# PEER in a two-layer diffusion step: rows run tile by tile, and table two's rows are summed two at a time in 64x64 tiles

## What is computed

```python
q = (xt @ wq).reshape(T, 8, 2, 128)                       # 8 heads, two halves
s1, s2 = q[:, :, 0] @ k1.T, q[:, :, 1] @ k2.T             # 128 scores each
v1, i1 = top_k(s1, 16); v2, i2 = top_k(s2, 16)
sc, pos = top_k(v1[..., :, None] + v2[..., None, :], 16)  # of 256 sums
eid = chosen i1 * 128 + i2; gate = softmax(sc)
act = gelu(sum_d x[t] * u_tab[eid])                       # table one
out[t] = sum over 8 heads x 16 of (gate * act) * v_tab[eid]   # table two
```

## Time and profile before

| what | us or share |
|---|---|
| median of the runs | 2608.44 |
| the profiled execution | 2606.61 |
| its span, first to last instruction | 2604.7 |
| PE, matmul busy | 2125.3 (82%) |
| DVE busy | 1598.7 (61%) |
| POOL busy | 948.2 (36%) |
| ACT busy | 486.4 (19%) |
| gathers (queue q0) | 805.36 MB, 74.7% of the 16 DMA engines' span |

### The profile page before, as it was taken

The page is one execution under the profiler, slowest core; times in us unless marked ns, Lnnn a source line. Parts: engine busy times, 40 slices in busy tenths (PEclk is TensorE's granted clock), DMA queues, the critical chain, the costliest instruction groups (busy, mean ns, idle before and its releaser), DMA issues.

```text
span 2604.7 us, 20351 instructions
## 1 busy us (share of the span) xinstructions
PE 2125.3 (82%) x6324; PEld 1044.5 (40%) x6324; DVE 1598.7 (61%) x4191; ACT 486.4 (19%) x1337; POOL 948.2 (36%) x775
## 2 busy tenths in 40 slices
PE   5998688697969787887899996797969688888777
PEld 2554433242424333433347654342424233334333
DVE  3234576767766677776432435777666677676764
ACT  2251211111111111111242112111111111111112
POOL 0000264444545444454100003544545444454541
PEclk9999699898989898998889997998989898999989
DMA  9993699999999999999723117999999999999994
GB/s 303 318 328 112 276 406 419 420 418 421 417 417 418 410 418 412 408 420 419 268 73 98 61 37 294 421 418 421 418 421 418 421 418 413 418 409 415 417 421 184
DMA packets 215769, 913.24 MB, mean 351 GB/s; under 512 B 19664, under 2 KB 116176, under 8 KB 116848
## 3 DMA queue, kind: packets, MB, share of 16 engines
q0 software_dynamic: 110592, 805.36, 74.7%
q1 hardware_dynamic: 97840, 101.20, 12.1%
q10 hardware_dynamic: 7232, 5.39, 0.7%
HBM read 909.26 MB, written 2.63 MB: 350 GB/s over the span
## 4 chain that ended last, share of the span: by engine, by line
PE 42%; DMA 41%; DVE 6%; POOL 5%; issue 3%; ACT 2%; SPq 0%; DVEq 0%; ACTq 0%
DMA slab<-in_peer_uv,idx 28%; PE psum L717 24%; PE psum L643 8%; DMA arena<-in_peer_uv,idx 8%; POOL slab L313 3%; POOL arena L313 2%; DMA slab<-in_ada_w 2%; DMA area<-in_peer_wq 2%; PE psum L681 2%; PE psum L819 2%; PE psum L608 2%; DVE slab L1077 2%; PE psum L897 1%; PE psum L758 1%; ACT diag L459 1%
## 5 line engine op out<-in xcount | busy, mean ns | idle before, releaser
L717 PE MATMUL psum<-arena,diag 128*128 128x512 f32 x2304 | 1087.6, 632 | 368.6 <-ACT diag L459 368.6
L313 POOL DMA_INDIRECT arena<-in_peer_uv,idx x576 | 698.9, 1213 | 1530.7 <-PE psum L717 879.6
L717 PEld LDWEIGHTS psum<-arena,diag 128*128 128x128 f32 x2304 | 459.9, 203 | 984.4 <-issue 984.4
L1077 DVE SCALAR_TENSOR_TENSOR arena<-arena,xtok 128x1024 f32<-128x1024 f32 x576 | 687.0, 1223 | 268.4 <-DMA arena<-in_peer_uv,idx 262.7
L1077 DVE SCALAR_TENSOR_TENSOR slab<-slab,xtok 128x1024 f32<-128x1024 f32 x192 | 235.4, 1228 | 227.4 <-DMA slab<-in_peer_uv,idx 227.4
L717 PE MATMUL psum<-slab,diag 128*128 128x512 f32 x768 | 337.4, 593 | 0.0
L313 POOL DMA_INDIRECT slab<-in_peer_uv,idx x192 | 245.3, 1278 | 71.5 <-issue 39.3
L459 ACT ACTIVATE diag<-ident,wts 128x128 f32<-128x128 f32 x768 | 235.0, 389 | 107.8 <-DVE wts L1098 107.4
L643 PE MATMUL psum<-arena,slab 128*128 128x384 f32 x672 | 227.8, 497 | 7.1 <-DVE arena L1147 4.9
L450 ACT ACTIVATE tanh<-inner 128x8 f32<-128x8 f32 (+1 forms) x98 | 20.3, 207 | 1140.5 <-DVE inner L1084 1140.5
L717 PEld LDWEIGHTS psum<-slab,diag 128*128 128x128 f32 x768 | 146.2, 190 | 183.4 <-issue 183.4
(11 more groups left out here) (222 smaller groups left out, 1482.2 us busy)
## 6 DMA issues: line engine op xcount, KB each, us to landing
slab<-in_ada_w SPq DMA_DIRECT2D x33, 1024.0 KB, 8.3
area<-in_peer_wq SPq DMA_DIRECT2D x16, 1024.0 KB, 25.4
slab<-in_gla_w_in SPq DMA_DIRECT2D x12, 1024.0 KB, 5.4
arena<-in_peer_uv,idx POOLq DMA_INDIRECT x576, 17.1
keys<-in_ada_w SPq DMA_DIRECT2D x8, 1024.0 KB, 9.2
area<-in_ada_w SPq DMA_DIRECT2D x7, 1024.0 KB, 7.7
slab<-in_rg_w_in SPq DMA_DIRECT2D x5, 1024.0 KB, 11.7
slab<-in_rg_w_out SPq DMA_DIRECT2D x4, 1024.0 KB, 8.8
```

Source lines behind the costliest of these rows:

```text
L313: pool.indirect_dma_start(row[n % RS], None, rows_of, bass.IndirectOffsetOnAxis(ap=rows[:, j:j + 1], axis=0)).then_inc(row_in[n % RS], 16)
L717: mm = pe.matmul(acc[t][:, half * 512:(half + 1) * 512], diag[j % DS][:, :], row[n % RS][:, D + half * 512:D + (half + 1) * 512], start=Fa ...
L1077: dve.scalar_tensor_tensor(row[n % RS][:, 0:D], row[n % RS][:, 0:D], 1.0, xtok[:, t * D:(t + 1) * D], ALU.mult, ALU.mult, accum_out=dots[t ...
```

## The change

The order of the blocks turns round: `t, h = divmod(b, PH)`, all eight heads of a tile, then the next tile. All heads' scores are now kept, in the slabs, so the ring loses their four places and has 12, all in `arena`. A part has 4 rows. Queries and scores are made two blocks ahead, in blocks 0 to 5. A diagonal matrix is now 128x64, one 64x64 diagonal over the other; two rows are multiplied together by eight products of 64 rows into 64 columns, in four different quarters of the array. They add to two sums of two banks that hold one tile. When a tile's 128 rows are done, ACT copies both sums, PE adds and transposes them in 16 products, and DVE adds the tile to the residual while the next tile runs. ACT's Gelu takes the place of tanh and of six small DVE operations a part. Three of the four first GLA slabs may now be loaded when the last block's rows have been chosen (`idx_ready` 24), the fourth after the last tile.

```diff
-RS, DS = 16, 8
-PARTS = (range(0, 8), range(8, 16))
+RS, DS = 12, 8
+PARTS = [range(4 * i, 4 * i + 4) for i in range(4)]
...
@@ SP
+                    if (name, j) == ("gla_in", 0):
+                        sp.wait_ge(sem("idx_ready"), NB)
+                    if (name, j) == ("gla_in", SLABS - 1):
+                        sp.wait_ge(sem("tile_mm"), NT)
...
-            sp.wait_ge(row_free, NB * TOPK)
             stream(PLACE["gla_in", 0], len(SEQ))
...
@@ ACT
+                def tile_sum(t):
+                    act.wait_ge(row_free, (layer * NB + PH * (t + 1)) * TOPK)
+                    act.wait_ge(sem("tile_mm"), NT * layer + t)
+                    for i in range(2):
+                        act.activation(total[:, i, :], acc[i], ACT.Copy).then_inc(sem("acc_ev"), 1)
...
                 queries(0, 1)
                 scores(0, 1)
+                queries(1)
+                scores(1)
                 exps(0)
-                exps(1)
...
+                    t, h = divmod(b, PH)
+                    if b + AHEAD < PH:
+                        queries(b + AHEAD)
+                    for i, part in enumerate(PARTS):
+                        if b == 0 and i == 1:
+                            exps(1)
+                        act.wait_ge(sem("dots_ready"), step)
+                        act.activation(gelu[r][:, p], dots[r][:, p], ACT.Gelu_apprx_tanh
+                                       ).then_inc(sem("gelu_ready"), 1)
+                        if i == 0 and b + AHEAD < PH:
+                            scores(b + AHEAD)
+                        act.wait_ge(sem("w_ready"), step)
                         for j in part:
...
+                            act.activation(diag[j % DS][:, :], ident2[:, :], ACT.Copy,
+                                           scale=wts[r][:, j:j + 1]).then_inc(sem("diag_ready"), 1)
...
@@ PE
                 queries(0, 1)
                 scores(0, 1)
+                queries(1)
+                scores(1)
+                def pair(b, j):
+                    n = (layer * NB + b) * TOPK + j
+                    for k in (0, 1):
+                        pe.wait_ge(row_in[(n + k) % RS], 16 * ((n + k) // RS + 1))
+                    pe.wait_ge(sem("diag_ready"), n + 2)
+                    for half in range(2):
+                        for k, i in ((0, 0), (0, 1), (1, 0), (1, 1)):
+                            a, o = HALF * i, HALF * (i ^ k)
+                            mm = pe.matmul(acc[i][o:o + HALF, half * 512:(half + 1) * 512],
+                                           diag[(j + k) % DS][a:a + HALF, :],
+                                           row[(n + k) % RS][a:a + HALF, D + half * 512:D + (half + 1) * 512],
+                                           start=False, stop=True, skip_group_check=True)
+                            if half == 1 and i == 1:
+                                mm.then_inc(row_free, 1)
...
+                clear()
                 for b in range(NB):
+                    t, h = divmod(b, PH)
+                    if b + AHEAD < PH:
+                        queries(b + AHEAD)
+                        scores(b + AHEAD)
+                    for j in range(0, TOPK, 2):
+                        pair(b, j)
+                    if h == PH - 1:
+                        turn(t)
...
@@ DVE
                 row_tops(0)
                 choose(layer, 0)
-                dve.wait_ge(sem("s_ev"), 2 * PH * layer + 2)
-                row_tops(1)
-                choose(layer, 1)
...
+                    dot(b, 0)
+                    if b > 0:
+                        weigh(b - 1, 3)
+                    for j in range(1, 4):
+                        dot(b, j)
...
+                    weigh(b, 0)
+                    if b == 0:
+                        dve.wait_ge(sem("s_ev"), 2 * PH * layer + 4)
+                        row_tops(1)
+                        choose(layer, 1)
+                    if ahead < NB:
+                        if ahead < PH:
+                            dve.wait_ge(sem("s_ev"), 2 * (PH * layer + ahead + 1))
+                        row_tops(ahead)
+                    for j in range(4, 8):
+                        dot(b, j)
                     if ahead < NB:
                         choose(layer, ahead)
+                    weigh(b, 1)
+                    for j in range(8, 13):
+                        dot(b, j)
+                    weigh(b, 2)
+                    if h == 1 and t > 0:
+                        add_tile(layer, t - 1)
+                    for j in range(13, 16):
+                        dot(b, j)
+                weigh(NB - 1, 3)
+                add_tile(layer, NT - 1)
```

More of the change, by code:

```diff
@@ L115, in build @@
         xT = sb("xT", [P, C, T])
-        slab = [sb(f"slab{i}", [P, C, SW]) for i in range(SLABS)]
+        slabs = sb("slabs", [P, SLABS * C * SW])
+        slab = [slabs[:, i * C * SW:(i + 1) * C * SW].rearrange("p (c n) -> p c n", c=C) for i in range(SLABS)]
         arena = sb("arena", [P, 8 * AW])
@@ L122, in build @@
         ident = sb("ident", [P, P])
+        ident2 = sb("ident2", [P, HALF])
         ones = sb("ones", [P, P])
@@ L203, in build @@
         dots = [sb(f"dots{i}", [P, TOPK]) for i in range(NT)]
-        inner = [sb(f"inner{i}", [P, TOPK]) for i in range(NT)]
-        tanh = [sb(f"tanh{i}", [P, TOPK]) for i in range(NT)]
+        gelu = [sb(f"gelu{i}", [P, TOPK]) for i in range(NT)]
         wts = [sb(f"wts{i}", [P, TOPK]) for i in range(NT)]
@@ L700, in peer, with clear @@
                 scores(0, 1)
+                queries(1)
+                scores(1)
+                def clear():
+                    for n in range(4):
+                        pe.matmul(bank[n], zrow[0:1, :], zrow[0:1, 0:1].to_broadcast([1, 512]), start=True, stop=True,
+                                  skip_group_check=True)
+                def pair(b, j):
[12 more added lines that the diff above has]
+                                mm.then_inc(row_free, 1)
@@ new lines, in turn @@
+                def turn(t):
+                    pe.wait_ge(sem("acc_ev"), 2 * (NT * layer + t + 1))
+                    if t < NT - 1:
+                        clear()
+                    if t > 0:
+                        pe.wait_ge(sem("tile_added"), (NT - 1) * layer + t)
+                    for c in range(C):
+                        for i in range(2):
+                            o = (c % 4) * P + HALF * i
+                            mm = pe.matmul(bank[4 + c // 4][:, o:o + HALF], total[:, i, c * P:(c + 1) * P], ident2[:, :],
+                                           start=True, stop=True, skip_group_check=True)
+                    mm.then_inc(sem("tile_mm"), 1)
@@ L1058, in residual_peer, with dot @@
                     dve.memset(wal, 0.0).then_inc(sem("wal_zero"), 1)
             def peer(layer):
+                def dot(b, j):
+                    t, r = b // PH, b % NT
+                    n = (layer * NB + b) * TOPK + j
+                    dve.wait_ge(row_in[n % RS], 16 * (n // RS + 1))
+                    ins = dve.scalar_tensor_tensor(row[n % RS][:, 0:D], row[n % RS][:, 0:D], 1.0,
+                                                   xtok[:, t * D:(t + 1) * D],
+                                                   ALU.mult, ALU.mult, accum_out=dots[r][:, j:j + 1])
+                    if j % 4 == 3:
+                        ins.then_inc(sem("dots_ready"), 1)
```

156 lines of the change are left out of this document (48 added, 108 removed).

## The result

The changed kernel takes 2721.5 us (median of 4 runs, 2718.7 to 2729.3), the kernel before 2607.1: 1.0444 times as long, 95% interval [1.0428, 1.0459]. Direction and range were right; the likeliest value, 2675, was 46 us short.

A forecast was written before the change was run, and what follows sets the result against it. DMA was taken to bound both PEER stages, so only their ends and added DMA count: 2606.6 + 67 (start) + 14.4 (GLA slabs) - 13.2 (tail) = 2675 us, range 2640 to 2735.

The forecast's parts named there:

- rival 1: PE's pairs: column halves take turns, 3.5 us a pair, 21 us a layer lost, 2717 us in all; chance 0.15.
- What bounds: Both PEER stages: DMA is full and PE is not; a stage costs 989 us wherever its rows are summed.
- The start: First block of each layer: two heads' queries before the first pair put rows 33.5 us behind, 67 for both layers.
- 15 x 2.49: Start of a layer: row 16 lands about when row 31 did, so fifteen rows at 2.49 us each are missing.
- Blocks 1 to 5: Blocks with look-ahead queries: a loop of 41.6 us against 44.6 of DMA, hidden with 3 us to spare.
- The pace and the slab: Gathers in PEER: a row lands every 2.49 us, a slab costs 4.8; three GLA slabs add 14.4 in layer 0.
- The tile boundaries: Between tiles: the sums of tiles 0 and 1 lie beside gathers and cost nothing.
- The tail: Last landing to ACT's last copy: 6.7 us, so 7.1 and 6.1 gained in the two layers; what follows stays even.
- Four quarters at once: PE's row products: all four array quarters run together, so a pair of rows takes 1.75 us.
- 2: PE's pairs: no overlap at all, 7.0 us a pair, PE sets the pace, near 3530 us; chance 0.02.
- 3: The ring of 12 starves: part 1 late by 2 us more than its slack, 96 us over 48 blocks, 2771; chance 0.06.
- 4: Gathers land faster with fewer full-height PE reads: decides from a pace of 2.40 us; 2572 us at 2.35; chance 0.05.

The follow-up runs named there:

- run 4: The changed kernel with rows summed by 128x128 diagonals and full products of one row by 512 columns, as in the kernel before: 2782.0 us.
- run 7: The changed kernel with only the clearing left between two tiles and the turning products moved behind the next tile's first eight rows: 2711.8 us.

## Why the prediction was right, and where it was short

The forecast's own uncertainty ended at 2700. The 2721 lies in the stated range only because that was widened for rival 1, whose cause the runs refute, and this part was luck. By its own steps, with the measured sum of 112 against its 68:

- **What bounds** was right in the steady stretches: DMA sets the pace there, and full products cost nothing from block 7 on (run 4). At the start, in blocks 1 to 5 and at the tile boundaries DMA is not full in the changed order, and there PE's price counts: run 4's 60 us.
- **The start** (67 us for both layers) was 79: 45.8 + 47.5 less two slabs of 3.5 in each. The forecast counted one more slab by row 31; it is two, four (heads 1 to 4) against two. Of layer 0's 5.3 us too little, 2.9 lie in row 16 (its dot at 377.5, not 372.9, less 1.7 ahead of the first gather), 1.3 in a slab taken off at 4.8, and 1.1 in the step "15 x 2.49" behind it, which took 42.0 us with a slab in it.
- **Blocks 1 to 5** ("hidden, with 3 us to spare") were not: the landing and half-clock pairs made the loop 44.9. Rows 31 to 95 cost 7.7 and 10.7 us more than two further slabs explain (three land there, before one). The step that failed took a part's pairs at the price of a busy PE and closed the loop without the row that DVE waits for.
- **The pace and the slab.** 2.49 came from 8 rows. Over 96 rows without slabs, 2329.39 to 2570.84 in layer 1 before, it is 2.515; after, 2445.77 to 2685.43, 2.496. With 2.515 the same 124.2 us leave 3.5 us for a slab, not 4.8. The three GLA slabs cost 7.6, not 14.4, 2.5 each. The Trainium skill ("DMA: Bandwidth & Descriptors", Specifications) states line rate for pieces of 512 B and more; by that a slab would cost 2.5 us. The GLA slabs agree, with the same 1 KB pieces; the query slabs, at 3.5, do not. Why these cost 1 us more stays open.
- **The tile boundaries** ("lie beside gathers and cost nothing") cost 5 to 6 us a layer: rows 95 to 351 should have gained 14 with four slabs fewer, and gained 8 to 9. By the prediction's own sign of being wrong, gaps in DMA after block 6, this step failed.
- **The tail** (13.2 gained) gained 6.0. Last dot to ACT's last copy was 1337.53 to 1345.65, but the 32 turning products took 5.26 us at a clock of 0.69 (3.79 in run 7, with the clock full) and the square sums 8.39 at 0.63, where "about 5.5" had been set.
- **Four quarters at once**, 1.75 us a pair, held at full clock: 1.83. The prediction took a rule of the Trainium skill ("TensorE: Matmul & The Clock Gate", Part 3), that weight loads overlap products in flight only when the row group differs, as speaking for rival 1. Here the products lie in two row groups and start 0.114 apart, against 0.437 for a 128x512 product: 3.8 times as often, where two row halves alone give 2. The measurement decides.
- **Rivals.** 1 and 2 fall by that pair and by run 4. 3 (the ring starves in every block) falls by the change's own blocks, 39.7 to 40.8 us from block 7 on apart from tile boundaries and GLA's slabs; in blocks 1 to 5 the loop does wait for a place and its landing, so there it holds in part. 4 falls: 2.496 does not reach its 2.40.

The sum of the misses: 12.3 + 18.4 + 11.2 - 6.8 + 8.9 = 44, the first being the start, the second blocks 1 to 5, the third the boundaries, the fourth GLA's slabs, the fifth tail and 1.7 us ahead of the first gather.

## What to carry to other kernels

Where transfers bound a stage, a cheaper sum gains nothing, and what buys it (a shorter ring, another order) is paid at each place where the queue runs dry; look there first, in windows of DMA share. Close a loop over in-order engines through every landing that an engine waits for, at the clock that an engine has after its pause, and put a copy that waits for a late transfer behind the work that does not need it. A pace is read over many periods: here one per cent of it made a slab look a third dearer than it is.

## What the runs showed of the hardware

Relieving TensorE lowered its clock: mean granted 0.92 before, 0.808 after, 0.895 with full products in the same order. Beside gathers that take 2.5 us for 1 MB in 8 KB pieces, 1 MB in 1 KB pieces cost 3.5 as a query slab and 2.5 as a GLA slab. A query slab took 25.7 us (median) to land in the kernel before, 26.6 at worst, and 5.4 in the change where the gathers had run out.
